# Encoder layer with expert-choice experts on one core: tile 8's sum and norm on ScalarE and GpSimd, last weight splits ahead of the final rows, and a new order of rounds, waves, norm sums and idle turns

## The chip, the cores and the metric

One core of a Trainium2 chip runs the whole layer in one launch. The metric is the device time of one execution in microseconds (us), lower is better; a version's time is the median of its runs.

## The reference, cut to what matters

```python
D_MODEL, SEQ, DEC_SEQ, N_EXPERTS, D_FF = 1024, 1024, 256, 16, 2816
h = rmsnorm(x, norm_mix)
u_b, u_c, u_x, u_f = split(h @ w_in)                  # 4 x 512 columns
y_conv = rmsnorm(short_conv_mixer(u_b, u_c, u_x), g_conv)   # gate, 3 taps, gate
y_four = rmsnorm(real(fft2(u_f, axes=(tokens, 64 channels))), g_fourier)
x = x + concat(y_conv, y_four) @ w_out
hn = rmsnorm(x, norm_ffn)
aff = softmax(hn @ w_router)                          # (tokens, 16)
gates, idx = top_k(aff.T, tokens // 8)                # each expert picks its tokens
x = x + scatter_add(idx, gates * (silu(hn[idx] @ w_gate) * (hn[idx] @ w_up)) @ w_down)
y = rmsnorm(x, norm_final)
```

It is computed for a request of 1024 tokens (128 picks per expert) and one of 256 tokens (32 picks), all in float32. The kernel treats them as 1280 rows, 10 tiles of 128.

## The kernel before, in words

**Precision.** A float32 product is three TensorE passes over a high part and a low part of each operand (`three`, L386 to L388). ScalarE writes the high part, VectorE the low part. The five engines run their own instruction lists, in order, and meet at semaphores.

**Start.** Tiles of x are squared, scaled and turned (transposed) on TensorE (`turn_x`, L1361); ScalarE copies the high part `hT_h` (L683) and splits `win` (L667). `project_ahead` (L1390) uses the first tiles before all have come. `win_raw` and x share one queue of SyncE.

**Projection.** Steps n = 2 to 15 each project 128 columns of u in eight k blocks (L1370). Between the k blocks TensorE has other work (`posts`): `waves(n - 3, 0..2)`, the Fourier step along the tokens, after k = 0, 1, 2, and `channels(n - 2, 0..4)` after k = 3 to 7. n = 6 has the last waves and no channels. `waves(j, 2)` are 12 narrow matmuls (at most 66 columns), and before each of `waves(j, 1)` and `waves(j, 2)` TensorE waits until VectorE has emptied bank 6 (L1012, L1013).

**Rows.** For each tile t, TensorE does `half(t, 0)` with the convolution weights `woc` and `half(t, 1)` with the Fourier weights `wof`, 24 matmuls each. `half(0, 1)` needs all of `wof_l` (L1066, semaphore `wol_ok`). For t = 0, ten pairs of one-column matmuls (`norm_sums`, L1442) run between the halves; from them come the norms `rn` (ScalarE L832, VectorE L1189), and with these ScalarE takes the first half out (`part`, L798). GpSimd adds x (`first_sum`, L543), VectorE adds the second half (`second_sum`, L1143), ScalarE squares and takes the root (L821, L823), VectorE inverts it and writes the normed rows (`normed`, L1149, L1153). TensorE turns these into `xnT` (`rows_turned(t - 1)`, L1499), between the halves of tile t. After tiles 0 to 3 and 4 to 7 (`GROUPS`) the router's logits, the softmax and its transpose follow (`router` L1511, `logits_turned` L1517, `group_turned` L1549); the third group, tiles 8 and 9, comes at the end.

**Picks.** VectorE finds the 128 largest of a list in 16 rounds of eight (`top(h, first, count)`: max L1133, index L1135, replace L1138). `top(0, ...)` works on tiles 0 to 3, `top(1, ...)` on tiles 4 to 7 and, from round 12 on, on the short request too, for which it waits for `A_ok` of the third group. Rounds are placed by hand between the VectorE work of tiles 4 to 9: arguments `early`, `late`, `after` of `rows`. Then lists are built, TensorE turns them (L1567), and GpSimd gathers the first expert's rows. While it does, TensorE runs `idle_turns` (L1540), transposes into bank 0 that nobody reads.

**Experts.** For each of 16 experts, 33 units of 1 MB of weights (22 for gate and up, 11 for down) go through 11 raw buffers and three split buffers (ScalarE L842, VectorE L1249, TensorE `three`). A split into a buffer waits until TensorE is done with the unit three before it. The short request's part (`sample_in`, L1618; `sample_down`, L1626) comes after units 5, 13, 21, 28 and 32; `ENDS` holds these.

**End.** Rows are read back (`load_rows`, L599), squared (L883), rooted (L888), scaled (VectorE L1283, L1285) and stored (`store_rows`, L603), each tile in its own `fx` buffer; semaphores are shared by tiles t and t + `FX`. `ROWS_STOP` and `ROWS_UNIT` say in which unit of the last expert ScalarE and VectorE do which tiles: 0, 1, 2 in unit 21, 3, 4, 5 in unit 28 (index b = 3 of `ENDS`), 6, 7 in unit 30 and 8, 9 in unit 31. ScalarE and VectorE do the split of unit i + 3 in their unit i, ahead of that unit's rows. GpSimd's list is: load 0 to 2; load 3 to 5; store 0 to 2; gather the last expert's rows; store 3 to 5; wait for `sample_down` of units 22 to 28; load 6 to 9; store 6 to 9. At the very end the last expert's rows are summed, normed (L1345, L940, L1350) and scattered (L641, L643).

Of the kernel before, what the change touches and what calls it, by code (L numbers as in the profile page):

```python
# [15 lines left out]
ALU = mybir.AluOpType  # L16
# [3 lines left out]
P = 128  # L20
# [41 lines left out]
FX = 6  # L62
ROWS_STOP = {2: (0, 1, 2), 3: (3, 4, 5)}
ROWS_UNIT = {INS + 8: (6, 7), INS + 9: (8, 9)}
# [3 lines left out]
PROJ = 4 * JH  # L68
PIECES = TILES // 2
# [8 lines left out]
def build(nc, x, norm_mix, w_in, conv_w, g_conv, g_fourier, w_out, norm_ffn, w_router, w_gate, w_up, w_down,  # L78
# [17 lines left out]
    with ExitStack() as ctx:  # L96
# [186 lines left out]
        x1_ok = sem("x1_ok")  # L283
        x2_ok = sem("x2_ok")
        ss_ok = sem("ss_ok")
# [12 lines left out]
        sx_ok = [sem(f"sx_ok{n}") for n in range(3)]  # L298
        ex_ok = [sem(f"ex_ok{n}") for n in range(3)]
        aT_ps = [sem(f"aT_ps{n}") for n in range(3)]  # L300
        A_ok = [sem(f"A_ok{n}") for n in range(3)]
# [197 lines left out]
        def _(pool):  # L499
# [48 lines left out]
            for t in range(TILES):  # L548
                if 1 <= t < TILES - 1:
                    stage_lo(t + 1, (t + 1) % 2)  # L550
                first_sum(t, t % 2)

# [68 lines left out]
            for t in range(3, FX):  # L621
                load_rows(t)
# [23 lines left out]
        def _(act):  # L646
# [136 lines left out]
            def group_exp(n):  # L783
                a, b = GROUPS[n]
                act.wait_ge(sx_ok[n], 2)
                act.activation(aff[:, 1, a:b, :], aff[:, 0, a:b, :], ACT.Exp).then_inc(ex_ok[n], 1)

            def group_rows(n):
                act.wait_ge(aT_ps[n], 1)
                act.wait_ge(pad_rt, 1)  # L790
                dst = (A0[:, :], A1[0:E, :], A1[32:32 + E, 0:DEC])[n]
                act.activation(dst, bank(7)[0:E, 0:(HALF, HALF, DEC)[n]], ACT.Copy).then_inc(A_ok[n], 1)
# [7 lines left out]
            def rows(t, s):  # L800
# [3 lines left out]
                if t < TILES and not ends:  # L804
                    part(t)
                if t >= 1:
# [142 lines left out]
        def _(dve):  # L949
# [155 lines left out]
            def group_shift(n):  # L1105
                a, b = GROUPS[n]
                dve.tensor_reduce(mx[:, a:b], aff[:, 0, a:b, :], AX_X, ALU.max).then_inc(sx_ok[n], 1)
                dve.wait_ge(sx_ok[n], 1)
                dve.tensor_tensor(aff[:, 0, a:b, :], aff[:, 0, a:b, :], mx[:, a:b].unsqueeze(2).broadcast_to([P, b - a, E]),
                                  ALU.subtract).then_inc(sx_ok[n], 1)  # L1110

            def group_share(n):
                a, b = GROUPS[n]
                dve.wait_ge(ex_ok[n], 1)
                dve.tensor_reduce(sm[:, a:b], aff[:, 1, a:b, :], AX_X, ALU.add).then_inc(sx_ok[n], 1)
                dve.wait_ge(sx_ok[n], 3)
                dve.reciprocal(mx[:, a:b], sm[:, a:b]).then_inc(sx_ok[n], 1)
                dve.wait_ge(sx_ok[n], 4)
                dve.tensor_tensor(aff[:, 2, a:b, :], aff[:, 1, a:b, :], mx[:, a:b].unsqueeze(2).broadcast_to([P, b - a, E]),
                                  ALU.mult).then_inc(sx_ok[n], 1)  # L1120

            def top(h, first, count):
                A, v, idx = ((A0, v0, i0), (A1, v1, i1))[h]
                dve.wait_ge(A_ok[h], 1)
                for r in range(first, first + count):
                    n = E
                    if h == 1 and r >= (CAP - CAPS) // 8:
                        n = 48
                        dve.wait_ge(A_ok[2], 1)
# [15 lines left out]

            def normed(t, s):
                dve.wait_ge(x2_ok, t + 2)
                dve.wait_ge(rt_ok, t + 1)
                dve.reciprocal(rr[:, 2 + s:3 + s], rt2[:, s:s + 1]).then_inc(rr_ok, 1)  # L1149
                dve.wait_ge(rr_ok, t + 1)  # L1150
                dve.wait_ge(nT_ps, t + 1)
# [10 lines left out]
            def rows(t, s, early, mid, between, late, after):  # L1162
# [54 lines left out]
            group_share(2)  # L1217
            top(1, 10, 6)
# [135 lines left out]
        def _(pe):  # L1354
# [84 lines left out]
            def norm_sums(q, col):  # L1439
# [314 lines left out]
```

## Time and profile before

| | us |
|---|---|
| median of 3 runs | 2486.88 (2484.79 to 2487.03) |
| the profiled execution | 2488.08 |
| its span in the trace | 2486.2 |
| TensorE busy in the span | 2424.6 (98%) |
| VectorE, ScalarE, GpSimd busy | 1611.8, 1358.4, 261.6 |
| mean granted clock of TensorE | 0.989 of full speed |

Durations and gaps are read from the profiled execution, whose span lies 1.9 us under its own time. Experts take from about 473 us to about 2470 us of the span; all parts that the change touches lie before and after that, and inside the last expert.

### The profile page before, as it was taken

The numbers are of one execution on the slowest core, as the hardware profiler recorded it, in microseconds if no ns is written. First come the engines' busy times: TensorE is split into PE (matmuls) and PEld (weight loads), VectorE is DVE, ScalarE is ACT, GpSimd is POOL, SyncE is SP. The second block draws the span as 40 slices with busy tenths as digits, with TensorE's granted clock in tenths as the row PEclk, the third lists the DMA queues.
The fourth block names the chain that finished last, engine by engine and source line by source line (L and its number), as shares of the span: only waits on it lengthen the run. The fifth ranks groups of instructions, "written<-read, shape, count | busy, mean of one in ns | idle before, by whom it ended". The sixth has DMA issues, their size and how long they took to land.

```text
span 2486.2 us, 45242 instructions
## 1 busy us (share of the span) xinstructions
PE 2424.6 (98%) x18368; PEld 1901.5 (76%) x18368; DVE 1611.8 (65%) x1331; ACT 1358.4 (55%) x1258; POOL 261.6 (11%) x234
## 2 busy tenths in 40 slices
PE   8999998699999999999999999999999999999996
PEld 7988887577777777777777777777777777777775
DVE  5443438766666666667666666666767676767665
ACT  6322343355555556565656565655555555555564
POOL 0020143102010202010201020102010101010102
PEclk9999999799999999999999999999999999999998
DMA  6002242568787878787878787878787878787877
GB/s 208 22 26 71 85 160 102 180 257 317 261 316 263 317 262 319 262 317 262 318 262 318 262 318 261 319 257 320 260 320 261 319 261 318 260 319 261 318 287 279
DMA packets 295966, 628.13 MB, mean 253 GB/s; under 512 B 21360, under 2 KB 72688, under 8 KB 295536
## 3 DMA queue, kind: packets, MB, share of 16 engines
q1 hardware_dynamic: 284160, 587.87, 64.2%
q0 software_dynamic: 11632, 37.51, 5.0%
q8 instruction: 161, 2.64, 0.4%
q14 instruction: 13, 0.11, 0.0%
HBM read 599.10 MB, written 26.21 MB: 252 GB/s over the span
## 4 chain that ended last, share of the span: by engine, by line
PE 92%; DVE 3%; issue 2%; DMA 1%; ACT 1%; POOL 0%; SPq 0%; POOLq 0%; DVEq 0%; ACTq 0%
PE ps L386 21%; PE ps L387 20%; PE ps L388 20%; PE ps L1618 12%; PE ps L1370 8%; PE ps L1626 6%; PE ps L1636 2%; DVE i L1135 1%; PE ps L1575 1%; DVE v L1133 1%; DVE A L1138 0%; PE ps L1390 0%; PE ps L1645 0%; DMA fx<-acc_dram 0%; DMA raw<-in_w_gate_dram 0%
## 5 line engine op out<-in xcount | busy, mean ns | idle before, releaser
L1249 DVE TENSOR_TENSOR spl_l<-raw,spl_h 128x2048 fp32r<-128x2048 f32 x528 | 1209.1, 2292 | 542.3 <-ACT spl_h L842 537.5
L842 ACT ACTIVATE spl_h<-raw 128x2048 fp32r<-128x2048 f32 x528 | 1011.8, 1917 | 583.6 <-PE ps L388 393.1
L386 PE MATMUL ps<-spl_h,xT 128*128 128x512 f32 x1408 | 554.1, 394 | 0.5 <-DVE xT L1254 0.4
L387 PE MATMUL ps<-spl_l,xT 128*128 128x512 f32 x1408 | 549.0, 390 | 0.0
L388 PE MATMUL ps<-spl_h,xT 128*128 128x512 f32 x1408 | 548.2, 389 | 0.0
L386 PEld LDWEIGHTS ps<-spl_h,xT 128*128 128x128 f32 x1408 | 264.2, 188 | 75.6 <-issue 19.1
L1618 PE MATMUL ps<-raw,xTs 128*32 128x256 f32 (+1 forms) x6144 | 314.2, 362 | 0.0
L388 PEld LDWEIGHTS ps<-spl_h,xT 128*128 128x128 f32 x1408 | 264.3, 188 | 56.1
L387 PEld LDWEIGHTS ps<-spl_l,xT 128*128 128x128 f32 x1408 | 264.3, 188 | 53.0
L386 PE MATMUL ps<-spl_h,g 128*128 128x512 f32 x704 | 279.1, 397 | 3.3 <-DVE spl_l L1249 3.3
L387 PE MATMUL ps<-spl_l,g 128*128 128x512 f32 x704 | 275.4, 391 | 0.0
L388 PE MATMUL ps<-spl_h,g 128*128 128x512 f32 x704 | 275.2, 391 | 0.0
L1618 PEld LDWEIGHTS ps<-raw,xTs 128*32 128x32 f32 x6144 | 189.4, 110 | 109.7 <-issue 8.1
L576 POOL DMA_INDIRECT acc_dram<-yP,sidx x15 | 28.9, 1929 | 1664.1 <-ACT yP L898 1664.1
L386 PEld LDWEIGHTS ps<-spl_h,g 128*128 128x128 f32 x704 | 132.6, 188 | 43.9 <-issue 12.8
L1626 PE MATMUL ps<-raw,gs 128*32 128x256 f32 x2816 | 158.9, 381 | 0.0
L388 PEld LDWEIGHTS ps<-spl_h,g 128*128 128x128 f32 x704 | 132.7, 189 | 28.4
L387 PEld LDWEIGHTS ps<-spl_l,g 128*128 128x128 f32 x704 | 132.7, 189 | 26.8
L1626 PEld LDWEIGHTS ps<-raw,gs 128*32 128x32 f32 x2816 | 88.2, 110 | 63.9 <-issue 8.9
L1370 PE MATMUL ps<-hT_h,win_h 128*128 128x256 f32 (+1 forms) x352 | 91.3, 359 | 0.0
L1370 PE MATMUL ps<-hT_h,win_l 128*128 128x256 f32 (+1 forms) x352 | 91.0, 358 | 0.0
L1370 PE MATMUL ps<-hT_l,win_h 128*128 128x256 f32 (+1 forms) x352 | 90.7, 357 | 0.0
(247 smaller groups left out, 1999.1 us busy)
## 6 DMA issues: line engine op xcount, KB each, us to landing
raw<-in_w_up_dram SPq DMA_DIRECT2D x352, 512.0 KB, 7.9
raw<-in_w_gate_dram SPq DMA_DIRECT2D x352, 512.0 KB, 9.3
raw<-in_w_down_dram SPq DMA_DIRECT2D x176, 1024.0 KB, 14.7
win_raw<-in_w_in_dram SPq DMA_DIRECT2D x16, 512.0 KB, 3.9
xt<-in_x_dram SPq DMA_DIRECT2D x10, 512.0 KB, 9.7
xr<-in_x_dram SPq DMA_DIRECT2D x10, 512.0 KB, 4.1
acc_dram<-xr SPq DMA_DIRECT2D x10, 512.0 KB, 2.7
xn_dram<-xn SPq DMA_DIRECT2D x10, 512.0 KB, 2.9
```

Of the source, the lines that this page charges most:

```text
L386: eng.matmul(o, a_h, b_h, start=first, stop=False, skip_group_check=True)
L387: eng.matmul(o, a_h, b_l, start=False, stop=False, skip_group_check=True)
L388: return eng.matmul(o, a_l, b_h, start=False, stop=last, skip_group_check=True)
L576: pool.indirect_dma_start(acc, bass.IndirectOffsetOnAxis(sidx[:, 0:1], 0), yP[:, :], None, compute_op=ALU.add).then_inc(added[0], 16)
L842: act.activation(spl_h[:, i % SPL, :], raw[:, slot_of(i), :], ACT.Copy).then_inc(sh_ok, 1)
L1133: dve.max(v[0:n, rs], A[0:n, :]).then_inc(top_ok[h], 1)
L1135: dve.max_index(idx[0:n, rs], v[0:n, rs], A[0:n, :]).then_inc(top_ok[h], 1)
L1249: dve.tensor_tensor(spl_l[:, i % SPL, :], raw[:, slot_of(i), :], spl_h[:, i % SPL, :].bitcast(F32), ALU.subtract).then_inc(sl_ok, 1)
L1370: last = pe.matmul(u[:, a:b], w[:, n % 2, k, :], h[:, k, a:b], start=(k == 0 and i == 0), stop=(k == KD - 1 and i == 2), skip_group_check= ...
L1618: last = pe.matmul(o, xTs[:, k, :], v_, start=k == 0, stop=k == KD - 1, skip_group_check=True)
L1626: last = pe.matmul(bank(6)[q * CAPS:(q + 1) * CAPS, 0:DQ], gs[:, f, :], raw[:, slot_of(i), b * D + q * DQ:b * D + (q + 1) * DQ], start=f = ...
L1636: last = pe.transpose(turned(c)[:, b, :], pv[:, c % 3, b * P:(b + 1) * P], ident[:, :])
```

## The change

- `idle_turns(24)` is put ahead of the first `turn_x`, `idle_turns(7)` behind the second; after the lists, `idle_turns(40)` and `(10)` become 50 and 14.
- At n = 6, `waves(3, 0..2)` run after k = 0, 2, 4.
- At t = 0, the norm sums run inside `half(0, 1)`: two columns before its k = 0, four before k = 1, four before k = 2. The wait for `wol_ok` now stands ahead of them.
- `rows_turned(t - 1)` moves from ahead of `half(t, 1)` to before its k = 3 block; in tiles 4 and 8 it stays ahead, in tile 9 it goes behind the half.
- Tile 8 (`AWAY`): ScalarE scales the second half into `x1t`, GpSimd adds it; ScalarE scales the row by the inverse root (which VectorE still takes), GpSimd multiplies by the gain.
- The rounds: fewer ahead of the norm of tiles 5 to 7, three of `top(0)` behind tile 7's norm, two of `top(1)` in tile 8.
- `FX` is 7; tiles 3, 4, 5 are squared and scaled in unit 29, behind the split of unit 32. GpSimd loads 6 to 9 ahead of storing 3 to 5.
- Four lists of three semaphores become four counted semaphores.

```diff
-FX = 6
-ROWS_STOP = {2: (0, 1, 2), 3: (3, 4, 5)}
-ROWS_UNIT = {INS + 8: (6, 7), INS + 9: (8, 9)}
+FX = 7
+ROWS_STOP = {2: (0, 1, 2)}
+ROWS_UNIT = {INS + 7: (3, 4, 5), INS + 8: (6, 7), INS + 9: (8, 9)}
+AWAY = TILES - 2
@@ gpsimd
                 first_sum(t, t % 2)
+                if t == AWAY:
+                    s = t % 2
+                    pool.wait_ge(x1_ok, t + 2)
+                    pool.wait_ge(x2_part, 1)
+                    pool.tensor_tensor(xr[:, s, :], xr[:, s, :], x1t[:, :], ALU.add).then_inc(x2_ok, 1)
+                if t == AWAY + 1:
+                    pool.wait_ge(xn_part, 1)
+                    pool.tensor_tensor(xn[:, AWAY % 2, :], xn[:, AWAY % 2, :], gffn[:, :], ALU.mult).then_inc(xn_ok, 1)
...
-            for t in range(3, FX):
+            for t in range(3, FX - 1):
                 load_rows(t)
...
-            for t in range(3, FX):
-                store_rows(t)
             pool.wait_ge(pe_s, (E - 1) * SAMPLE + NC + 1)
-            for t in range(FX, TILES):
+            for t in range(FX - 1, TILES):
                 load_rows(t)
-            for t in range(FX, TILES):
+            for t in range(3, TILES):
                 store_rows(t)
@@ scalar, rows(t, s)
+                if t == AWAY + 1:
+                    act.wait_ge(rr_ok, t)
+                    act.activation(xn[:, 1 - s, :], xr[:, 1 - s, :], ACT.Copy, scale=rr[:, 3 - s:4 - s]).then_inc(xn_part, 1)
                 if t >= 1:
                     act.wait_ge(nT_ps, t + 2)
...
+                if t == AWAY:
+                    act.wait_ge(of_done, t + 3)
+                    act.wait_ge(x1_ok, t + 2)
+                    act.activation(x1t[:, :], bank(2, 2), ACT.Copy, scale=rn[:, 1, t:t + 1]).then_inc(x2_part, 1)
                 if t < TILES:
                     act.wait_ge(x2_ok, t + 2)
@@ vector
+            def root_inverse(t, s):
+                dve.wait_ge(rt_ok, t + 1)
+                dve.reciprocal(rr[:, 2 + s:3 + s], rt2[:, s:s + 1]).then_inc(rr_ok, 1)
...
+                if t == AWAY + 1:
+                    dve.wait_ge(xn_ok, t + 2)
...
-                second_sum(t, s)
+                if t != AWAY:
+                    second_sum(t, s)
                 if after:
                     top(*after)
-                normed(t, s)
+                if t != AWAY:
+                    normed(t, s)
+                else:
+                    root_inverse(t, s)
...
-            rows(5, 1, (0, 1, 3), None, None, (0, 4, 1), (0, 5, 1))
-            rows(6, 0, (0, 6, 2), None, None, (0, 8, 1), (0, 9, 1))
-            rows(7, 1, (0, 10, 3), None, None, (0, 13, 1), (0, 14, 1))
-            top(0, 15, 1)
+            rows(5, 1, (0, 1, 3), None, None, None, (0, 4, 1))
+            rows(6, 0, (0, 5, 3), None, None, None, (0, 8, 1))
+            rows(7, 1, (0, 9, 3), None, None, None, (0, 12, 1))
+            top(0, 13, 3)
...
-            rows(8, 0, None, None, None, None, (1, 0, 1))
-            rows(9, 1, (1, 1, 3), None, None, (1, 4, 1), (1, 5, 1))
-            top(1, 6, 3)
+            rows(8, 0, None, None, None, None, (1, 0, 2))
+            rows(9, 1, (1, 2, 2), None, None, None, (1, 4, 1))
+            top(1, 5, 5)
             group_logits(2)
             group_shift(2)
-            top(1, 9, 1)
+            top(1, 10, 1)
             group_share(2)
-            top(1, 10, 6)
+            top(1, 11, 5)
@@ tensor
+            idle_turns(24)
             for t in range(2):
                 turn_x(t)
+            idle_turns(7)
...
-                    if 3 <= n < 3 + JH and k < 3:
-                        waves(n - 3, k)
+                    at = (0, 2, 4) if n == 2 + JH else (0, 1, 2)
+                    if 3 <= n < 3 + JH and k in at:
+                        waves(n - 3, at.index(k))
...
                 if t == 0:
                     pe.wait_ge(qs_ok, JH - 1)
                     pe.wait_ge(rn_rt, 1)
-                    norm_sums(qc, 0)
                     pe.wait_ge(wol_ok, KD)
+                    between = {0: lambda: norm_sums(qc, 0, 0, 2), 1: lambda: norm_sums(qc, 0, 2, 6),
+                               2: lambda: norm_sums(qc, 0, 6, TILES)}
+                elif ends:
+                    rows_turned(t - 1)
+                    between = {1: lambda: router(ends[0]), 2: lambda: logits_turned(ends[0])}
+                elif t == AWAY + 1:
+                    between = {}
                 else:
-                    rows_turned(t - 1)
+                    between = {3: lambda: rows_turned(t - 1)}
...
+                half(t, s, 1, of_done, between)
+                if t == AWAY + 1:
+                    rows_turned(AWAY)
...
-            idle_turns(40)
+            idle_turns(50)
             gathered(1)
-            idle_turns(10)
+            idle_turns(14)
```

## Rows read from the trace of the kernel before

**Rows 1.** The page, part 1: busy time and share of each engine
```profile
PE 2424.6 (98%) x18368; PEld 1901.5 (76%) x18368; DVE 1611.8 (65%) x1331; ACT 1358.4 (55%) x1258; POOL 261.6 (11%) x234
```

**Rows 2.** Timeline of the start (start, us, engine, line, what, [idle before <- releaser])
```profile
7.57 3.65 PE L1361 MATMUL ps<-ident,xs 128*128 128x128 f32 x16 [7.57 <-DVE xs L958]
12.49 2.08 PE L1390 MATMUL ps<-hT_h,win_h 128*128 128x256 f32 x8 [1.28 <-ACT hT_h L683]
...
14.89 1.97 PE L1361 MATMUL ps<-ident,xs 128*128 128x128 f32 x8 [0.33 <-DVE xs L958]
...
22.84 1.12 PE L1390 MATMUL ps<-hT_l,win_h 128*128 128x256 f32 x8
```

**Rows 3.** Timeline at the last narrow waves
```profile
157.34 0.30 PE L386 MATMUL ps<-tsm,Y_h 128*128 128x66 f32 x1 [0.92 <-DVE yfour L1013]
```

**Rows 4.** One-us window: PE, PEld, DVE, ACT, POOL busy, clock, DMA
```profile
159.00:160.00 1.00, 1.00 (x4) 0.82 (x3) 0.62 (x4) 0.24 (x2) 0.02 (x1) 0.50 0.00 0
```

**Rows 5.** Timeline of tile 0
```profile
303.56 2.50 PE L1442 MATMUL ps<-ones,qc 128*128 128x1 f32 x20
...
312.97 0.39 PE L386 MATMUL ps<-woc_h,ysh 128*128 128x512 f32 x1
...
306.09 0.27 ACT L832 ACTIVATE rm<-ps,eps 128x10 f32<-128x10 f32 x1 [3.55 <-PE ps L1442]
...
308.93 1.12 ACT L798 ACTIVATE x1t<-ps,rn 128x1024 f32<-128x1024 f32 x1 [1.53 <-issue]
...
301.54 4.24 DVE L1066 SCALAR_TENSOR_TENSOR wof_l<-wof_raw,gm,wof_h 128x1024 fp32r<-128x1024 f32 x2 [2.38 <-ACT wof_h L744]
```

**Rows 6.** Waits of PE, 40 to 500 us: total, times, longest
```profile
PE ps L1499 <- DVE xn L1153: 8.4, 3, 5.0
```

**Rows 7.** Timeline of the rounds and tile 8, VectorE, ScalarE, GpSimd, TensorE
```profile
368.26 0.68 DVE L1133 MAX8 v<-A 16x8 f32<-16x512 f32 x1
...
370.53 0.68 DVE L1133 MAX8 v<-A 16x8 f32<-16x512 f32 x1
...
413.65 0.23 DVE L1159 COPY aff<-ps 128x64 f32<-128x64 f32 x1 [3.69 <-PE ps L1517]
...
417.68 0.67 DVE L1133 MAX8 v<-A 16x8 f32<-16x512 f32 x1
...
418.97 1.28 ACT L823 ACT_TABLE_LOAD   x1
...
410.85 2.38 POOL L543 TENSOR_TENSOR xr<-xr,x1t 128x1024 f32<-128x1024 f32 x1 [0.97 <-ACT x1t L798]
...
461.80 0.34 PE L1567 MATMUL ps<-ident,vals 48*128 48x48 f32 x1 [14.54 <-DVE idxf L1238]
```

**Rows 8.** Timeline of the first gather, TensorE
```profile
462.28 6.44 PE L1540 MATMUL ps<-ident 128*128 128x128 f32 x40
...
469.79 1.09 PE L1575 MATMUL ps<-ident,xg 128*128 128x128 f32 x8 [1.07 <-DMA xg<-xn_dram,idxT]
```

**Rows 9.** Timeline of the end, TensorE, ScalarE, VectorE, GpSimd
```profile
2442.30 6.25 PE L1626 MATMUL ps<-raw,gs 128*32 128x256 f32 x112
...
2460.28 0.79 PE L386 MATMUL ps<-spl_h,g 128*128 128x512 f32 x1 [3.30 <-DVE spl_l L1249]
...
2454.00 1.90 ACT L842 ACTIVATE spl_h<-raw 128x2048 fp32r<-128x2048 f32 x1
...
2467.95 1.03 ACT L883 ACTIVATE ps<-fx 128x1024 f32<-128x1024 f32 x1 [0.31 <-DMA fx<-acc_dram]
...
2469.33 1.01 ACT L883 ACTIVATE ps<-fx 128x1024 f32<-128x1024 f32 x1
...
2472.25 1.28 DVE L1345 SCALAR_TENSOR_TENSOR accP<-ps,cgate,accP 128x1024 f32<-128x1024 f32 x1
...
2458.84 2.12 POOL L599 DMA_DIRECT2D fx<-acc_dram  x4
```

**Rows 10.** Two-us window while the last weights land (last column GB/s)
```profile
2448.00:2450.00 2.00, 2.00 (x19) 1.31 (x12) 2.00 (x2) 1.91 (x5) 0.00 (x0) 1.00 1.01 412
```

More of the change, by code:

```diff
@@ L283, in build @@
         x1_ok = sem("x1_ok")
+        x2_part = sem("x2_part")
         x2_ok = sem("x2_ok")
+        xn_part = sem("xn_part")
         ss_ok = sem("ss_ok")
@@ L297, in build @@
         lg_ok = sem("lg_ok")
[L298 to L301, printed above, removed]
+        sx_ok = sem("sx_ok")
+        ex_ok = sem("ex_ok")
+        aT_ps = sem("aT_ps")
+        A_ok = sem("A_ok")
         pad_rt = sem("pad_rt")
@@ L1128, in top @@
                         n = 48
-                        dve.wait_ge(A_ok[2], 1)
+                        dve.wait_ge(A_ok, 3)
                     rs = slice(8 * r, 8 * r + 8)
@@ L1437, in waves, with norm_sums, idle_turns @@
                 last.then_inc(ds_done, 1)
-            def norm_sums(q, col):
-                for t in range(TILES):
+            def norm_sums(q, col, a=0, b=TILES):
+                for t in range(a, b):
                     last = pe.matmul(bank(7)[:, col + t:col + t + 1], q[:, t * P:(t + 1) * P], ones[:, 0:1],
                                      start=True, stop=True)
-                last.then_inc(nrm_ps, 1)
+                if b == TILES:
+                    last.then_inc(nrm_ps, 1)
+            def idle_turns(count):
+                for _ in range(count):
+                    pe.transpose(bank(0)[:, 0:P], ident[:, :], ident[:, :])
             pe.wait_ge(ident_ok, 4)
+            idle_turns(24)
             for t in range(2):
                 turn_x(t)
+            idle_turns(7)
             project_ahead(0, 0, 256, 2, {(0, 7): 2, (1, 7): 3})
@@ L1523, in rows @@
                 half(t, s, 0, oc_done)
+                ends = [n for n in range(2) if t == GROUPS[n][1]]
                 if t == 0:
@@ L1526, in rows @@
                     pe.wait_ge(rn_rt, 1)
-                    norm_sums(qc, 0)
                     pe.wait_ge(wol_ok, KD)
+                    between = {0: lambda: norm_sums(qc, 0, 0, 2), 1: lambda: norm_sums(qc, 0, 2, 6),
[5 more added lines that the diff above has]
+                    between = {}
                 else:
-                    rows_turned(t - 1)
+                    between = {3: lambda: rows_turned(t - 1)}
                 pe.wait_ge(ysl_ok, t * 2 + 2)
                 pe.wait_ge(x2_ok, t + 1)
-                ends = [n for n in range(2) if t == GROUPS[n][1]]
-                half(t, s, 1, of_done, {1: lambda: router(ends[0]), 2: lambda: logits_turned(ends[0])} if ends else {})
+                half(t, s, 1, of_done, between)
+                if t == AWAY + 1:
+                    rows_turned(AWAY)
                 for n in ends:
                     group_turned(n)
-            def idle_turns(count):
-                for _ in range(count):
-                    pe.transpose(bank(0)[:, 0:P], ident[:, :], ident[:, :])
             def group_turned(n):
                 a, b = GROUPS[n]
-                pe.wait_ge(sx_ok[n], 5)
+                pe.wait_ge(sx_ok, 5 * n + 5)
                 pe.wait_ge(rn_rt, 2)
                 if n:
-                    pe.wait_ge(A_ok[n - 1], 1)
+                    pe.wait_ge(A_ok, n)
                 for t in range(a, b):
                     last = pe.transpose(bank(7)[0:E, (t - a) * P:(t - a + 1) * P], aff[:, 2, t, :], ident[:, :])
-                last.then_inc(aT_ps[n], 1)
+                last.then_inc(aT_ps, 1)
             pe.wait_ge(wol_ok, JH)
```

31 lines of the change are left out of this document (15 added, 16 removed).

## The prediction

> **What bounds the kernel now.** I read the page first: TensorE is busy 98% of the span, the others 65% or less [rows 1]. So a cheaper VectorE or ScalarE operation brings nothing in the middle; what can be won is TensorE's idle time and its time at the lower clock. The windows and the timelines then show where these lie: the start; one gap at n = 6; tile 0 of the rows; the routing, in which TensorE waits for VectorE; and the end, where rows are finished behind the last matmul. The experts, some 2000 us between, are untouched, and I count nothing there.
>
> **Part 1, idle turns at the start.** TensorE's first instruction starts at 7.57 [rows 2]. 24 turns at the 0.23 us of the first sixteen (3.65 / 16) take 5.5 us and fit ahead of it. The first groups run slow: eight 256-column matmuls take 2.08 at 12.49 and 1.12 at 22.84, and the turn of tile 2 takes 1.97 [rows 2]. With TensorE busy beforehand I expect the fast rate from 12.49 on. Then the turn of tile 2 and the eight matmuls behind it save 0.9 and 1.0, and ScalarE, which copies what the next turn leaves and then splits the next weights, moves up with them. Bounds 0 (another input is late) and -1.9; I take **-1.6**.
>
> **Part 2, waves at n = 6.** Now TensorE waits 0.92 for VectorE ahead of the narrow matmuls [rows 3], 1.1 with the pipeline's restart, and right after them the granted clock is 0.50, that is 1.2 GHz [rows 4], for about 3.4 us (three such windows and parts of two), which loses 1.7. With another projection block between, VectorE is done in time, and narrow waves stand between full matmuls, as in n = 3 to 5, where the clock stays at 2.4 GHz. Bounds 0 and -2.8; I take **-2.7**. VectorE's short waves come some 3 us later; nobody needs them for tens of us.
>
> **Part 3, tile 0.** The norm sums take 2.50 from 303.56 [rows 5], and after them, from 305.7 to 309.1, the windows show 0.50 as in [rows 4] again (-1.6 if they did not). The last `wof_l` split ends at 301.54 + 4.24 = 305.8 [rows 5]; so far the sums cover that wait. Now the wait stands ahead of them: TensorE idles 303.5 to 305.8, and the sums then lengthen the half. The half took 306.06 to 312.97 [rows 5], 5.4 without the 1.6 lost to the clock, 1.35 a block. The sums end at 305.8 + 2.5 + 2 x 1.35 = 311.0 instead of 306.06. From the root at 306.09 to the end of `x1t` at 308.93 + 1.12 it is 4.0 [rows 5], with two row copies, their low parts and the inverse between; so `x1t` is ready at 315.0, while the half ends at 305.8 + 2.5 + 5.4 = 313.7. TensorE idles another 1.3, and tile 1 starts at 315.0 instead of 312.97: **+2.0** if the clock holds, **+3.6** if it falls. The idle stretch with two sums behind it is 2.8 long, the one after which it fell 2.5; I hold the fall for likelier. Three units of weights are asked for 5 us later, but are split over 100 us after.
>
> **Part 4, tiles 1 to 7.** Moving the turn behind three blocks (4.1 us) removes TensorE's two waits for the norms of tiles 5 and 7: 8.4 - 5.0 = 3.4 [rows 6]; the third, of 5.0, is tile 9's. **-3.4.** In tile 8 the turn stays ahead, but only one round now stands between tile 7's sum and its norm. The three rounds moved behind the norm (two of 2.27 [rows 7], one shorter) and the conversion fill VectorE's idle 3.69 ahead of the logits [rows 7] and overrun it by a few tenths. VectorE's removed second sum gives 0.1. The list of tiles 4 to 7, and with it `top(1, 0)`, now at 417.68 [rows 7], comes 1.5 earlier, or 0.1 later with a clock fall.
>
> **Part 5, tile 8 and the last rounds.** From there the 16 rounds of VectorE set the end: TensorE waits 14.5 for the lists [rows 7]. Removed: tile 8's norm 1.3 and the waits about it 0.9: -2.2. Added: the inverse, 0.2, and its wait. ScalarE now copies 1.0 and GpSimd adds 2.38 [rows 7] before the square can start, 3.5 later than now; the table load of 1.28 [rows 7] and the root follow, to about 424.1 in the old frame. VectorE has done its two rounds at 417.5 + 2 x 2.27 = 422.1 and stands 2.0. Then tile 9: GpSimd adds (2.38), multiplies (2.4), TensorE turns tile 8, ScalarE copies that, and only then squares tile 9; VectorE reaches tile 9's inverse some 1.4 early and stands again. Sum -2.2 + 0.2 + 2.0 + 1.4 = **+1.4**. Bounds: -2.0 (no stall) and +3. So moving 2.5 us away from VectorE brings nothing, because VectorE then waits in the same place. Routing in all: +3.6 - 3.4 - 0.1 + 1.4 = **+1.5** with the fall, -0.1 without. The merged semaphores count in the order in which they are used: 0.
>
> **Part 6, 50 and 14 turns.** 40 took 6.44, and 1.07 was free before the gathered rows landed [rows 8]. The late ones go fast, so ten more cost 1.1 to 2.3. Four more hide behind the split of the gathered rows by all but a tenth. Bounds 0 and +4; **+0.2**.
>
> **Part 7, the end.** `sample_down` ends at 2442.30 + 6.25 = 2448.55, unit 29 is done at 2451.3, and the split of unit 32 could start; it starts at 2454.00, behind tiles 3 to 5, and TensorE waits 3.30 for it [rows 9]. Now it starts at 2451.4 and ends at 2453.3. Rows 6 to 9 are asked for at 2448.6 instead of 2458.84 [rows 9], since their loads no longer queue behind three stores; they are there before ScalarE wants them. So the end is a ScalarE chain: 2453.3, one table load, seven tiles at 2469.33 - 2467.95 = 1.4 [rows 9], to 2464.4; VectorE ends tile 9 at 2466.0, and the last expert's sum starts there instead of at 2472.25 [rows 9]: **-6.2**. TensorE is long done, at about 2463. Stores go out each 1.4 us. Bounds: -2 (loads delay the weights of unit 32) and -7.
>
> What decides this term is whether unit 32's weights are there at 2451.4. Around 2449 the rings move 412 GB/s [rows 10], and this ends by 2451. If all four loads (2.1 MB) went ahead of them, they would come up to 5.1 us late, ScalarE's whole list behind them, and only about 2 would be left. The Trainium skill says (DMA: Bandwidth & Descriptors, section Queues, rings and completion order) that each DMA engine takes turns between queues, a packet each. By that, at most 0.5 MB of unit 32 would be slowed to half speed, an estimate of 1.2 us at most; no row here shows the two queues apart.
>
> **The sum.** -1.6 - 2.7 + 1.5 + 0.2 - 6.2 = -8.8. The profiled execution took 2488.08 and would take 2479.3; it lies 1.2 above the median, so for a median I say 2486.88 - 8.9 = **2478.0**.
>
> **The rivals.**
> - *No clock fall in tile 0*, since the sums are scattered: -10.5, **2476.4**. For it: the two waits of tiles 5 and 7, 3.4 together [rows 6], passed without one. Against it: this one is longer.
> - *The end is bound by DMA*, as under part 7: -2 instead of -6.2, **2482.2**. Against it: the weights were asked for 22 us earlier.
> - *The front gives nothing and the tail stalls more*: parts 1 and 2 at 0, part 5 at +3: 2478.0 + 4.3 + 1.6 = **2483.9**, the same within 0.2% (5 us, about what a measurement of this kernel can tell from no change).
> - *The change does not do what it says* for tile 8: that is my forecast. That split 32 moves up less than thought, for ScalarE is held by unit 31, would give 2480 to 2482; against it, ScalarE already does tiles 3 to 5 between the two splits.
> - *Slower*: the clock, once down in tile 0, stays down while idle gaps follow (the 1.3 ahead of tile 1). Each us of full-rate work then costs one more; from 8.9 us of such work on, the gains are gone, from 14 on it is visible; through tiles 0 and 1 (some 20 us) it gives **2496**. Against it: after both falls in this stretch the clock came back in 3.4 us of dense work.
>
> **How the numbers follow.** Chances: forecast 0.45, no fall 0.27, end bound by DMA 0.12, front and tail 0.11, slower 0.05. The forecast, the second case and half of the third lie below 2481.9, with a little of the fourth: faster 0.82; same 0.14; slower 0.04. The range runs from 2474.0 (no fall, and VectorE not stalled) to 2483.0, which leaves out the slower case and half of the fourth.
>
> **What would show each step.** Start: the turn of tile 2 takes 1.0. n = 6: no 0.50 window. Tile 0: TensorE idle some 2.3 ahead of the second half, 1.3 ahead of tile 1, with or without a 0.50 window. Tiles 5 to 7: no wait at L1499. Tile 8: VectorE idle 2.0 and 1.4 at the two inverses, and the lists 1.5 later against `top(1, 0)`. End: split 32 some 2.6 earlier, no 3.30 wait on TensorE, seven tiles at 1.4 each, the sum 6 us earlier. I am wrong if split 32 waits for DMA, if VectorE's stalls in tile 8 are missing, or if a gap appears in the first expert.

## The result, and the profile after

The kernel after takes **2565.88 us** (median of 4 runs, 2563.18 to 2570.17) against 2486.84 (2484.79 to 2487.03): ratio 1.0321, 95% interval 1.0303 to 1.0339, 79 us slower. The prediction said 2478.0 and gave "slower" 0.04. The profiled execution took 2570.17 us, span 2568.3. The page's busy times, clock by 40 slices, DMA queue of the instructions, and the start of the chain:

```profile
PE 2453.3 (96%) x18413; PEld 1925.5 (75%) x18413; DVE 1615.5 (63%) x1329; ACT 1362.9 (53%) x1260; POOL 211.5 (8%) x236
...
PEclk9999899899999999999999999999999999999998
...
q8 instruction: 161, 2.64, 0.4%
...
PE 87%; issue 5%; DMA 3%; DVE 2%; ACT 2%; SPq 1%; POOL 0%; POOLq 0%; ACTq 0%; DVEq 0%
```

Against [rows 1], TensorE is busy 28.7 us longer, with 45 more matmuls (the idle turns), and idle 53.4 us longer. "issue" in the chain was 2% before; it is time in which an engine waits for nothing that the profile shows. The waits of TensorE in the experts (500 to 2470 us; total, times, longest) have one row, which the kernel before does not have:

```profile
PE ps L389 <- issue: 58.4, 13, 4.6
```

Thirteen is the number of times the loop over the experts jumps back (14 passes; the first and last expert stand outside it). The timeline of TensorE at the first jump, before:

```profile
718.64 3.66 PE L1626 MATMUL ps<-raw,gs 128*32 128x256 f32 x64
722.23 0.50 PE L386 MATMUL ps<-spl_h,xT 128*128 128x512 f32 x1
```

and after, with VectorE's split of the first unit that the new pass multiplies:

```profile
719.94 2.29 DVE L1274 TENSOR_TENSOR spl_l<-raw,spl_h 128x2048 fp32r<-128x2048 f32 x1 [0.43 <-ACT spl_h L858]
...
723.32 3.66 PE L1663 MATMUL ps<-raw,gs 128*32 128x256 f32 x64
731.31 0.79 PE L389 MATMUL ps<-spl_h,xT 128*128 128x512 f32 x1 [4.33 <-issue]
```

The last `sample_down` of a pass ends at 726.98; the next pass begins 4.33 later. The split that it needs is done at 722.23 (splits run three units ahead; those that follow, at 722.94 and 726.46, are for the second and third unit), so the whole wait is nobody's. Behind each gap the clock falls as well. Two-us windows (busy PE, PEld, DVE, ACT, POOL; granted clock; DMA share; GB/s):

```profile
728.00:730.00 2.00, 0.00 (x0) 0.00 (x0) 0.75 (x1) 0.00 (x0) 1.64 (x3) 0.77 1.05 384
730.00:732.00 2.00, 0.69 (x2) 0.60 (x3) 0.00 (x0) 0.00 (x0) 1.12 (x4) 0.50 1.09 288
732.00:734.00 2.00, 2.00 (x6) 1.57 (x5) 0.00 (x0) 0.00 (x0) 1.39 (x2) 0.50 1.04 244
734.00:736.00 2.00, 2.00 (x6) 1.59 (x5) 0.00 (x0) 0.00 (x0) 0.00 (x0) 0.52 1.11 332
736.00:738.00 2.00, 2.00 (x10) 1.61 (x10) 0.00 (x0) 1.52 (x1) 0.54 (x4) 1.00 1.03 412
```

At 0.50 (1.2 GHz) the 512-column matmuls start 0.43 us apart instead of 0.23. The gap costs 4.33 to 4.6, the clock behind it some 2, and an expert takes 130.9 us instead of 124.4.

Three stretches account for the whole. First expert's first `sample_in` and the last `sample_down` ahead of the final rows, before (the latter stands in [rows 9]):

```profile
490.23 5.41 PE L1618 MATMUL ps<-raw,xTs 128*32 128x128 f32 x128
```

and after:

```profile
494.92 5.41 PE L1655 MATMUL ps<-raw,xTs 128*32 128x128 f32 x128
...
2530.68 6.25 PE L1663 MATMUL ps<-raw,gs 128*32 128x256 f32 x112
```

To the first expert +4.7 (predicted -2.6, the sum without part 7); the experts 2035.8 against 1952.1, **+83.7** (predicted 0); from there to the end of the span 37.6 against 43.9, -6.3 (predicted -6.2). Together +82.1, the difference of the spans.

**Tile 0.** The timeline of TensorE, and windows (columns as above):

```profile
306.30 0.99 PE L1467 MATMUL ps<-ones,qc 128*128 128x1 f32 x4 [2.44 <-issue]
309.85 1.70 PE L1467 MATMUL ps<-ones,qc 128*128 128x1 f32 x8
314.12 1.70 PE L1467 MATMUL ps<-ones,qc 128*128 128x1 f32 x8
```

```profile
306.00:308.00 2.00, 1.70 (x6) 1.64 (x7) 0.09 (x1) 0.00 (x0) 0.00 (x0) 0.50 0.03 12
...
316.00:318.00 2.00, 2.00 (x6) 1.52 (x6) 0.81 (x2) 1.16 (x3) 0.00 (x0) 0.50 0.44 63
318.00:320.00 2.00, 2.00 (x7) 1.63 (x6) 0.61 (x2) 1.12 (x1) 0.02 (x1) 0.63 1.08 382
```

TensorE idles 2.44 as foretold (2.3), but the clock stays at 0.50 for 13 us instead of 3.4, so the sums end at 315.8, not 311.0, and tile 1 starts at 320.27 instead of 312.97, 7.3 us later.

**n = 6.** No 0.50 window is left there, and TensorE's step and with it VectorE's product behind it (`yconv`, L1073, 1057 before) come 2.7 us earlier (166.64 against 169.30). But the split of the next weights, which now starts earlier, takes longer. VectorE, after:

```profile
169.20 12.62 DVE L979 SCALAR_TENSOR_TENSOR win_l<-win_raw,gmix,win_h 128x128 fp32r<-128x128 f32 x8 [1.00 <-ACT win_h L676]
```

and before:

```profile
171.85 8.11 DVE L963 SCALAR_TENSOR_TENSOR win_l<-win_raw,gmix,win_h 128x128 fp32r<-128x128 f32 x8 [0.99 <-ACT win_h L667]
```

Beside it GpSimd squares the waves' result, in seven operations, and these start later than before, since the waves do (162.4 to 180.9; before 160.0 to 178.5). In the traces' single records one of the eight pieces of the split takes 0.34 with GpSimd at rest and 2.5 to 3.1 where it starts together with one of GpSimd's operations (2.3 and 3.0): five pieces are held like this after, three before. The Trainium skill (SBUF — State Buffer) says that the two engines share a pair of ports and lock each other out; the 12.62 for 8.11 us agree. So the split ends at 181.82, later than before (179.96), and now TensorE waits for it, which at this place it does not in before:

```profile
181.87 0.85 PE L1395 MATMUL ps<-hT_h,win_h 128*128 128x512 f32 x3 [1.19 <-DVE win_l L979]
```

### The profile page after: what moved, and what is told of

It is laid out like the page before. It is cut to its first block, busy times and chain, and to the rows that moved or that the text cites. A ratio compares the mean times of both kernels' runs of the same rounds, so it can differ in the third digit from the quotient of the medians.

```text
span 2568.3 us, 45331 instructions
## 1 busy us (share of the span) xinstructions
PE 2453.3 (96%) x18413; PEld 1925.5 (75%) x18413; DVE 1615.5 (63%) x1329; ACT 1362.9 (53%) x1260; POOL 211.5 (8%) x236
## 4 chain that ended last, share of the span: by engine, by line
PE 87%; issue 5%; DMA 3%; DVE 2%; ACT 2%; SPq 1%; POOL 0%; POOLq 0%; ACTq 0%; DVEq 0%
PE ps L389 20%; PE ps L390 19%; PE ps L391 19%; PE ps L1655 12%; PE ps L1395 8%; PE ps L1663 4%; DMA raw<-in_w_gate_dram 3%; PE ps L1673 1%; DVE spl_l L1274 1%; ACT spl_h L858 1%; DVE win_l L979 1%; PE ps L1612 1%; PE ps L1415 0%; PE ps L1682 0%; SPq L443 0%
## 5 line engine op out<-in xcount | busy, mean ns | idle before, releaser
L389 PE MATMUL ps<-spl_h,xT 128*128 128x512 f32 x1408 | 564.8, 401 | 59.2 <-issue 58.4
L390 PE MATMUL ps<-spl_l,xT 128*128 128x512 f32 x1408 | 558.4, 397 | 0.0
L391 PE MATMUL ps<-spl_h,xT 128*128 128x512 f32 x1408 | 557.5, 396 | 0.0
L389 PEld LDWEIGHTS ps<-spl_h,xT 128*128 128x128 f32 x1408 | 270.7, 192 | 136.4 <-issue 79.6
L391 PEld LDWEIGHTS ps<-spl_h,xT 128*128 128x128 f32 x1408 | 270.0, 192 | 58.2
L390 PEld LDWEIGHTS ps<-spl_l,xT 128*128 128x128 f32 x1408 | 270.9, 192 | 55.5
L389 PE MATMUL ps<-spl_h,g 128*128 128x512 f32 x704 | 278.0, 395 | 0.0
L389 PEld LDWEIGHTS ps<-spl_h,g 128*128 128x128 f32 x704 | 132.1, 188 | 40.0 <-issue 13.2
L869 ACT ACTIVATE sv<-ps 128x512 f32<-128x512 f32 (+1 forms) x96 | 54.0, 563 | 73.6 <-PE ps L391 73.5
```

What stands on the lines that cost most here:

```text
L389: eng.matmul(o, a_h, b_h, start=first, stop=False, skip_group_check=True)
L390: eng.matmul(o, a_h, b_l, start=False, stop=False, skip_group_check=True)
L391: return eng.matmul(o, a_l, b_h, start=False, stop=last, skip_group_check=True)
L869: act.activation(sv[:, 0:blocks(c) * P], gate_bank(c), ACT.Silu).then_inc(s_ok, 1)
```

## The experiments

Before-runs shared these chips, median 2487.3 to 2487.9. In TensorE's compiled program the loop is 2,059 instructions from its first to the jump (the traces have 2,058 records a pass) and the same in all kernels; **s** is how many instructions it stands later than in after. An idle turn is two instructions (a load of weights and a matmul). In before, s is -89.

### Is it the program's length ahead of the loop?

```diff
-            idle_turns(24)
...
-            idle_turns(7)
...
-            idle_turns(50)
+            idle_turns(40)
...
-            idle_turns(14)
+            idle_turns(10)
```

> The kernel after with the idle turns of before: none at the start (24 and 7 left out), 40 and 10 ahead of the experts; TensorE's program ahead of its loop over the experts is 45 turns shorter, the loop itself the same. Theory A (the place at which the loop's instructions stand in TensorE's program decides whether the jump back stalls): the 13 idle times of 4.6 us at the loop's start go, 2565.9 - 13 x (130.9 - 124.4) = 2565.9 - 84.5 = about 2481, with 2478 to 2487. Theory B (another part of the change, the shared semaphores or the order on VectorE and ScalarE, delays the first unit of each expert): the 13 stalls stay and the time is within 3 us of 2566.

2484.80 (10 runs), ratio to before 0.9989 (0.998 to 0.9999). No stall. The reverse, before with these four turn counts of after:

> The kernel before with the idle turns of after alone (24 and 7 at the start, 50 for 40 and 14 for 10 ahead of the experts); nothing else is changed. Theory A: the 13 stalls of 4.6 us and the expert period of 130.9 us appear here too, 2486.9 + 84.5 = about 2571 (2566 to 2574). Theory B: no stall, 2487 within 3 us.

2569.86 (4 runs), ratio 1.0328 (1.0311 to 1.0345), and `PE ps L386 <- issue: 58.1, 13, 4.5` among the waits. So the turns alone make the loss, and nothing else of the change is needed. Between the two, with the first two lines of the diff only, and with the last two only:

> The kernel after without the 24 and 7 idle turns at the start; the 50 and 14 ahead of the experts stay. The loop stands 31 turns (62 instructions) earlier than in after and 14 turns (28 instructions) later than in before. Theory A says only that it is one of the two levels, near 2481 without the stalls or near 2566 with them, and this run tells on which side of the switch 14 turns lie. If a stall instead grows with the count (rival A2, a smooth effect of the program's length), it is near 2481 + 14/45 x 84.5 = 2507. Theory B: 2566.

> The kernel after with 40 and 10 idle turns ahead of the experts and the 24 and 7 at the start kept. The loop stands 14 turns (28 instructions) earlier than in after, 31 turns later than in before. Theory A: near 2481 or near 2566, and with the run before it this brackets the switch. Rival A2: 2481 + 31/45 x 84.5 = 2539. Theory B: 2566.

2489.93 (ratio 1.0013, 1.0003 to 1.0023), no stall; and 2543.50 (1.0231, 1.0214 to 1.0248). (after_front_old lies 5.1 above after_old_turns, from which it differs by the 14 turns ahead of the experts; in the one profile of each the first expert starts 12.43 against 12.16 behind the lists, and the experts take 1958.5 against 1952.5. Why is open.) In after_back_old the stall stands elsewhere. TensorE at the first jump of after_back_old:

```profile
722.19 0.50 PE L389 MATMUL ps<-spl_h,xT 128*128 128x512 f32 x1
...
723.90 0.39 PE L390 MATMUL ps<-spl_l,xT 128*128 128x512 f32 x1
727.14 0.50 PE L391 MATMUL ps<-spl_h,xT 128*128 128x512 f32 x1 [2.85 <-issue]
```

The pass begins without a gap, does 8 matmuls and then stands, between two matmuls of the same unit of weights, until 4.95 after its first one. TensorE waits for no semaphore there; what is left is the instruction list. (Where the loop is left there is one more wait, of 3.9, and of 2.5 in tile0_front24 below.) That gave theory A1: the list comes in blocks; the block **behind** the jump's target is asked for at the jump, the **target's own** when TensorE enters the last block ahead of the jump, and each is there some 4.9 us later. The border lies behind the 8th matmul for s = -28; for s = 0 it lies ahead of the loop's first instruction, and (the loop is 8 blocks and 11 instructions long, if a block is 256) 17 instructions ahead of the jump. The Trainium skill (Runtime: NRT & Kernel Launch, section Instruction fetch mechanics) has the size: 256 instructions, fetched by DMA while the block before runs, and a taken branch out of the window "forces a DMA fetch of the target page before execution can continue". By that alone every jump would stall, also in before; there none does. The loop carries a hint of its jump (`hint_back_edge`), and A1 puts the early request down to it; a run without the hint was not made.

### A1 against a smooth effect

More instructions ahead of the loop, as waits on a semaphore long set (two of them make one instruction):

```diff
+            for _ in range(260):
+                pe.wait_ge(ident_ok, 4)
             idle_turns(50)
```

> The kernel after with 130 more instructions in TensorE's program ahead of its loop over the experts (waits on a semaphore that is long set, ahead of the 50 idle turns, where TensorE waits for the gather); the loop then stands 130 instructions later than in after, where it stalled by 4.5 us per pass. Theory A1 (the program is fetched in blocks of a fixed number of instructions; the block that the jump leads to is asked for when TensorE enters the last block ahead of the jump, and comes some 4.9 us later; only the position inside a block decides): from a block's border to the jump there are now some 147 instructions, the 64 short matmuls of 3.66 us and some 9 of 0.23 us, 5.8 us in all, more than 4.9 us: no stall, period 124.4 us, time 2485 to 2497 (2485 with the old turns, and up to 10 us for the added instructions). Theory A2 (the longer the program ahead of the loop, the longer the stall): 2566 or more.

2495.71 (5 runs), ratio 1.0034 (1.0021 to 1.0047), **no stall**, first expert at 502.5 instead of 494.9 for the waits themselves. A program longer than after's is 70 us faster. With 120 in place of 260:

> The kernel after with 60 more instructions ahead of the loop in the same way. A1: some 77 instructions from the border to the jump, 38 short matmuls or 2.2 us, so 4.9 - 2.2 = a stall of about 2.7 us at the first matmul of each pass, and with the clock that falls behind it some 4 us per pass: 2485 + 13 x 4 + 5 = about 2540 (2525 to 2550). A2: over 2566.

2544.57 (2 runs), `PE ps L389 <- issue: 41.4, 13, 3.3`. Without the 7 turns alone:

> The kernel after without the 7 idle turns behind the first two turns of x; the loop stands 14 instructions earlier. A1: the border lies between the loop's first instruction and its third matmul or so, and 3 instructions ahead of the jump. The block of the jump's target is then late by some 4.8 us, and the block behind it is wanted at once too. If both are asked for together, the stall stays about 4.8 us and the time near 2566 (2562 to 2572); if one is asked for after the other, there are two stalls per pass, up to 9.5 us together, and the time is up to 2485 + 13 x 11 = 2628. A2: between the runs with 28 instructions fewer (2543.5) and none (2565.9), about 2555.

2570.80 (2 runs), `PE ps L389 <- issue: 60.9, 13, 4.8`, one gap and not two. Last, on the kernel tile0_old below, 24 turns at the start and nothing else (s = -42):

> The run tile0_old (2478.0, no stall at the loop) with 24 idle turns at the start, which put the loop 47 instructions later, 14 earlier than in after_back_old, where the stall was 2.85 us ahead of the 9th matmul. A1 (a block border at a fixed place of the list, the next block there 4.95 us after the jump): the stall moves to the 16th matmul of each pass and shrinks to 4.95 - 3.73 = about 1.2 us; with what the clock adds 1.2 to 2.5 us per pass, 2478 + 13 x 1.2..2.5 = 2494 to 2510. A2 (a smooth effect of the number of instructions) does not move the stall to another matmul.

2505.24 (2 runs). Its first jump:

```profile
717.58 0.50 PE L389 MATMUL ps<-spl_h,xT 128*128 128x512 f32 x1
...
720.66 0.39 PE L390 MATMUL ps<-spl_l,xT 128*128 128x512 f32 x1
722.70 0.40 PE L391 MATMUL ps<-spl_h,xT 128*128 128x512 f32 x1 [1.65 <-issue]
```

The stall is ahead of the 15th matmul (foretold: the 16th; one instruction in between is no matmul), 5.12 after the first, and is 1.4 to 1.8 long, 1.5 in the mean of the 13. In one table, in order of s:

| s | kernel | stall | where | us |
|---|---|---|---|---|
| -89 | before; after_old_turns | none | | 2487; 2484.8 |
| -61 | after_front_old | none | | 2489.9 |
| -42 | tile0_front24 | 1.5 | 15th matmul | 2505.2 |
| -28 | after_back_old | 2.9 | 9th matmul | 2543.5 |
| -14 | after_minus7turns | 4.7 | 1st | 2570.8 |
| 0 | after; before_new_turns | 4.5 | 1st | 2565.9; 2569.9 |
| +60 | after_plus60 | 3.2 | 1st | 2544.6 |
| +130 | after_plus130 | none | | 2495.7 |

The two sides answer to A1's two requests: left of the border the work between jump and border counts (14 matmuls cover 3.5 of 5.1), right of it the work between border and jump (77 instructions cover some 2 of 5). Before stands less than 50 instructions from the first stall.

**The traces have the fetches themselves.** They are packets of 16,384 bytes on the queue that the page calls "q8 instruction", 9 in each pass of the loop in every kernel, in before too: the loop is fetched anew each time, and what differs is only when a block is wanted. The traces also have the jump instruction, which no view shows. At the first jump:

| kernel | jump: start, us | packets, after the jump's start | TensorE goes on at |
|---|---|---|---|
| before | 720.94, 0.39 | 3.79 | does not stop |
| after_back_old | 720.90, 0.39 | 3.79 | 6.24 |
| tile0_front24 | 716.29, 0.39 | 3.76 | 6.41 |
| after | 725.62, **5.24** | 2.65 | 5.69 |
| after_plus60 | 726.22, **4.02** | 1.42 | 4.47 |
| after_plus130 | 733.20, 0.39 | -5.08 and 3.81 | does not stop |

A packet takes 1.05 us, and TensorE goes on 1.4 to 2.0 behind its end. In the second and third row it is the block behind the target that is late, in the fourth and fifth the target's own, for which the jump itself is held. One thing of A1 stays open: after_minus7turns should need two blocks at once, but its trace has one packet, 2.96 behind the jump's start (5.56 long), and the next at 8.89.

### The parts of the change, without the stall

All have the old turn counts. Tile 0's norm sums in one piece ahead of the half, as before:

```diff
+                    norm_sums(qc, 0)
                     pe.wait_ge(wol_ok, KD)
-                    between = {0: lambda: norm_sums(qc, 0, 0, 2), 1: lambda: norm_sums(qc, 0, 2, 6),
-                               2: lambda: norm_sums(qc, 0, 6, TILES)}
+                    between = {}
```

> The kernel after with the idle turns of before (no stall at the loop) and tile 0's norm sums in one piece ahead of its half 1, as in before. Theory C (the sums scattered through half 1 at half clock cost tile 0 time, as the profile of after shows): the first expert starts some 2 us earlier than in the run with the old turns alone (492.3), and the time is 2 to 3 us less than its 2484.8, about 2482.5. Rival: what tile 0 loses is a matter of which stretches get the low clock, which falls out differently with every edit; 2484.8 within 1.5 us.

**2478.01** (5 runs, 2475.27 to 2481.37), ratio 0.9959 (0.9946 to 0.9973): faster than both. Against after_old_turns 6.8 less. Two windows of its profile, behind the sums:

```profile
308.00:310.00 2.00, 2.00 (x7) 1.58 (x7) 1.27 (x3) 0.65 (x1) 0.00 (x0) 0.68 0.94 306
310.00:312.00 2.00, 2.00 (x11) 1.63 (x10) 0.00 (x0) 0.47 (x1) 1.36 (x1) 1.00 1.10 365
```

It is back at 1.00 by 310; with the scattered sums it comes back at 319. On this kernel, the waves at n = 6 at k = 0, 1, 2:

> The run tile0_old (2478.0) with the waves at n=6 at k = 0, 1, 2 as in before. The prediction's part 2 says 2.7 us: 2480.7. The profile of after shows that the split of win_l takes 12.6 for 8.1 us behind it and that only 1.2 us of the 2.7 are left at the first norm sums: 2479.2. If nothing is left in the end: 2478 within 1 us.

2478.03 (6 runs), 0.9964 (0.9951 to 0.9976): **nothing** is left of the 2.7 (each ratio is known to some 3 us). Tile 8 back on VectorE (`AWAY = 2 * TILES`):

> The run tile0_old (2478.0) with tile 8's second sum and norm back on VectorE, the order of the rounds left as in after. The prediction's part 5 counts tile 8 and the last rounds at +1.4 us for the change, so 1 us less here: about 2477 (2475 to 2478.5). Rival (moving it away from VectorE does help, since the rounds behind it start earlier): 2479 to 2481.

2476.24 (4 runs), 0.9955 (0.9938 to 0.9972), and once more, with more rounds:

> The run tile0_vec8_old (2476.24, 4 runs) once more with more rounds, as the version to keep: 2476.2 within 1.5 us, ratio to before 0.9955.

2475.79 (5 runs), 0.9952 (0.9939 to 0.9966): 2 us lower both times, as part 5 said, though the intervals overlap that of tile0_old. This is the version to keep, 11.8 us faster than before and 90 faster than after. The old end on tile0_old (`FX = 6`, rows 3 to 5 at stop 3, GpSimd's old list):

> The run tile0_old (2478.0) with the end of before (rows 3 to 5 split at the third stop of the last expert, six buffers, their stores ahead of the last loads). The prediction's part 7 says that the end of after is worth 6.2 us and the two profiles show 23.70 against 17.45 us from the last sample_down to the last gather's row: 2484.2 (2482 to 2487). Rival: part of the 6.2 us was hidden, under 2481.

2479.03 (6 runs), 0.9969 (0.9956 to 0.9981): only 1.0 slower. So I put the new end alone on before, took before again, and this one again:

> The kernel before with the end of after alone (seven buffers, rows 3 to 5 behind the last split, their stores behind the last loads). Prediction (part 7): 2487.5 - 6.2 = 2481.3 (2480 to 2483). If the run tile0_end_old was right that the end is worth 1.0 us in the median (3.0 us by its profile, 40.65 against 37.6 us from the last sample_down to the end): 2484.5 to 2486.5.

> The kernel before once more, unchanged, for a second profile of its end. Theory D (the last weights land in another order from run to run, so that the profile on which part 7 was worked out had a late landing in it: ScalarE waited 5.83 us ahead of the last two splits of stop 3, and 3.2 us in every kernel since): this profile has a wait near 3.2 us, some 20.4 us from the end of the last sample_down of stop 3 to the last gather's row instead of 23.70. Rival (it belongs to the kernel): 5.8 us and 23.7 us again.

> The run tile0_end_old once more: D says its 20.41 us from the last sample_down to the last gather's row may come out at 23.7 in this profile as well, else 20.4; the time 2479 (2478 to 2484).

before_end_new: 2480.44 (8 runs), 0.9971 (0.996 to 0.9981), **-7.1**. before_again: 2486.44, its last splits wait 5.81 again and the last sum starts 24.2 behind the `sample_down`; theory D falls. end_old_again: 2480.91 (7 runs), wait 3.29 on ScalarE, as in its first profile (3.21). So the same end is worth 7.1 on one base and 1.0 to 2.9 on the other, and the difference is in the code.

### ScalarE's border

ScalarE's last splits ahead of the final rows, in before:

```profile
2436.37 1.92 ACT L842 ACTIVATE spl_h<-raw 128x2048 fp32r<-128x2048 f32 x1 [0.80 <-PE ps L388]
2444.12 3.72 ACT L842 ACTIVATE spl_h<-raw 128x2048 fp32r<-128x2048 f32 x2 [5.83 <-issue]
```

and in tile0_end_old, where ScalarE's program is three instructions longer ahead of the loop:

```profile
2428.20 1.92 ACT L860 ACTIVATE spl_h<-raw 128x2048 fp32r<-128x2048 f32 x1 [0.80 <-PE ps L391]
2433.32 5.52 ACT L860 ACTIVATE spl_h<-raw 128x2048 fp32r<-128x2048 f32 x3 [3.21 <-issue]
```

The same kind of wait, for nothing shown, one split earlier. Before with only these instructions added (6 waits in place of one for 3 instructions, 24 for 12):

```diff
-            act.wait_ge(ident_ok, 3)
+            for _ in range(3 * 2):
+                act.wait_ge(ident_ok, 3)
             act.activation(rt2[:, 0:1], eps[:, 0:1], ACT.Sqrt)
```

> The kernel before with 3 more instructions at the start of ScalarE's program (waits on a semaphore that is long set). In the profiles so far ScalarE waits at the end for nothing the profile shows: 5.8 us and then two splits where its program has the length of before (before, before_again, before_end_new, tile0_vec8_old, best_again), 3.2 us and then three splits where tile 8's two operations make it 3 instructions longer (after, tile0_old, tile0_end_old, end_old_again). Theory E (this too is a block border in the list of instructions): with the 3 instructions alone the wait becomes 3.2 us and three splits follow, the last sample_down of stop 3 to the end of the span takes 40.7 instead of 43.9 us, and the time is 2487.5 - 3.2 = 2484.3. Rival (tile 8's order or other code does it): 5.8 us, two splits, 2487.5.

> The same with 12 more instructions. E: the wait stands some 4 splits' instructions earlier than in before, ahead of a split that is not wanted so soon, and the last sample_down to the end takes 40.7 us or less. Rival: as before, 43.9 us.

before_act3: **2483.09** (10 runs), 0.998 (0.9971 to 0.999):

```profile
2432.18 1.92 ACT L843 ACTIVATE spl_h<-raw 128x2048 fp32r<-128x2048 f32 x1 [0.80 <-PE ps L388]
2437.36 5.52 ACT L843 ACTIVATE spl_h<-raw 128x2048 fp32r<-128x2048 f32 x3 [3.25 <-issue]
2440.84 6.25 PE L1627 MATMUL ps<-raw,gs 128*32 128x256 f32 x112
```

Three idle instructions at the start of ScalarE's program make the kernel 4.6 us faster. From its `sample_down` to the end of the span it is 2481.5 - 2440.8 = 40.7, as expected. With 12, 2483.39, 0.9983 (0.9973 to 0.9993), no such gap is left among the last seven splits, and the tail is 2480.9 - 2440.4 = 40.5. Here too the traces have the fetch: a packet of 8,192 bytes on "q14 instruction" starts at 2442.48 in before, 2431.62 in tile0_end_old and 2435.66 in before_act3, each inside the wait, which ends 1.6 to 1.7 later; with 12 it comes at 2422.21, ahead of the splits. Why this block is asked for only when it is wanted was not tried; in these stretches the DMA rings move 406 to 412 GB/s. The new end makes the wait harmless: from `sample_down` to the end of the span it is 37.6 in before_end_new, where ScalarE stands 5.89, and in tile0_old, where it stands 3.21; the old end takes 43.9 and 40.6.

## Why the prediction was wrong

- **"The experts, some 2000 us between, are untouched, and I count nothing there" failed**, and is nearly the whole error: 83.7 us of 88 (2565.9 - 2478.0). The code of the loop is untouched; its place is not. Part 1 and part 6 counted the turns' own time and nothing else, though the diff says that TensorE's program grows by 45 turns ahead of the loop. What the runs showed in its place: with these turns alone TensorE stands 4.5 us at each of 13 jumps for a block of its instructions, and the lower clock behind it costs 2 more. None of the rivals had it; "slower" was put at 0.04 and on the clock in tile 0. The sign "if a gap appears in the first expert" came near: the gaps stand ahead of the third to the fifteenth.
- **Parts 1 and 6** (-1.6, +0.2): in after the turns run as planned, but the eight matmuls at 12.42 still take 2.08: TensorE stands 2.16 ahead of them for ScalarE's `hT_h`, and the clock is at 0.50 from there, where before it was at 1.00 (so what made these eight slow before was not the granted clock). At the end of the group at 22.86 nothing is gained (22.84 before). The first expert starts 1.3 earlier in before_new_turns than in before, one profile each, against 2 to 3 us of scatter between profiles whose front is the same code. The turns' price without the stall stays open.
- **Part 2** (-2.7): the step itself came as said, and the run without it says 0.0. What failed is "nobody needs them for tens of us": GpSimd does, and its later squares hold VectorE's split (12.62 for 8.11), for which TensorE now waits 1.2; and a new 0.50 stretch of 3.4 us at 220 to 224 costs 1.7. Both are in the profiles of after and tile0_old, neither in that of tile0_waves_old.
- **Part 3** (+3.6): right in kind, too small: 6.8 between after_old_turns and tile0_old, 7.3 at tile 1's start between the profiles of before and after. The step that failed is the length of the fall, 3.4 us in the sum and 13 in the profile. The prediction's slower rival named this mechanism; it was no case of its own but part of what happened. The idle 1.3 ahead of tile 1 did not come, since the half ended later.
- **Part 4** (-3.4): the waits for tiles 5 and 7 are gone as said (1.80 and 1.58 before), and of the third, 5.0, 1.97 ahead of tile 8's turn and 1.88 ahead of tile 9's are left, which is part 5's matter. Its size is what is left of before to tile0_old: -9.3 (2487.3 - 2478.0) = -7.1 (end) + 2.0 (tile 8) + 0 (waves) + part 4, so -4.2, an estimate from medians of which each is known to some 3 us.
- **Part 5** (+1.4): right, 1.8 and 2.2 in two runs; VectorE stands 1.80 and 1.54 at the two inverses (2.0 and 1.4 foretold).
- **Part 7** (-6.2): right on before, -7.1, and by after's profile, -6.3. Split 32 starts at 2540.01 and the rows follow each 1.37. But the 3.30 wait that it removes was no cost of the rows ahead of the split: with ScalarE's border moved by three instructions the rows still stand there, the wait is gone, and 4.6 of the 7.1 (3.2 by the profiles) are there without the new end. That the number came out right is in this part luck.

Without the turns, the change as made gives -3.1 (after_old_turns) where parts 2 to 5 and 7 said -7.4.

## What to carry to other kernels

Code ahead of a loop whose instructions are fetched anew in each pass (here 9 packets for 2,059 instructions) is not free even where its time is hidden: after every edit look for "issue" waits that come once per pass, and shift the loop by some tens of instructions if they are there, before judging the edit. An edit's size is only known once its neighbours' borders are held fixed; compare with a padded base. Filler that keeps a clock up is worth having only where the profile shows that nothing but the clock makes the next work slow.

## What was unexpected of the hardware

- A jump back with a hint costs nothing or up to 4.8 us, by the loop's place alone. Its instructions come as 16,384-byte packets, 9 a pass with or without a stall; the block behind the target is there 4.95 to 5.12 us after the pass's first matmul (after_back_old, tile0_front24), the target's own, by A1's count, some 5 us from the entry into the jump's block. A gap of 2.9 us costs (2543.5 - 2489.9) / 13 = 4.1 a pass with the clock behind it; one of 1.5 costs (2505.2 - 2478.0) / 13 = 2.1, or 1.6 by the mean length of a pass in the two profiles (126.23 and 124.61).
- ScalarE, in straight code, stands 3.2 or 5.8 us at such a place near the end of the span, with an 8,192-byte packet of instructions landing inside the wait; 3 added instructions are worth 4.6 us.
- A VectorE operation of 0.34 us takes 2.5 to 3.1 when it starts together with a GpSimd operation of 2.3 to 3.0; a later GpSimd operation so moved a split that TensorE waits for.
- The clock in tile 0 stayed at 0.50 for 3.4 us behind 2.5 or 2.6 us of one-column matmuls in one piece (before, tile0_old), and for 13 us where the same matmuls stood in three groups between blocks of wide ones.
